# Twelve weight slabs a layer multiplied as 2x2 blocks with seven block products (Strassen's scheme), the block sums on GpSimd

## What is computed

```python
h = rms_norm(x, norm_g)
proj = h @ w_in                       # 1024 columns in, 7496 out
(sa_q, sa_k, sa_v, c_q, c_kv, k_pe, ds_q, ds_k, ds_v, ix_q, ix_k, ix_w,
 z_a, z_b, z_c, g) = jnp.split(proj, _split_points(IN_SIZES), axis=-1)
# y_a, y_b, y_c: three kinds of attention on the first twelve pieces
branches = jnp.stack([y_a * jax.nn.silu(z_a), y_b * jax.nn.silu(z_b), y_c * jax.nn.silu(z_c)], axis=2)
up = jnp.einsum('bsnc,ncd->bsnd', branches, w_branch)
gates = jax.nn.sigmoid(g.reshape(B, S, N_BRANCH, D) + gate_b)
merged = jnp.sum(gates * up, axis=2)
return x + merged @ w_out
```

## Time and profile before

| | |
|---|---|
| median of three runs | 1280.16 us (1278.92 to 1280.26) |
| the profiled execution's own time | 1282.07 us |
| its span in the profile | 1280.3 us |
| granted TensorE clock, share of full | 0.999 |
| TensorE, VectorE, ScalarE, GpSimd busy | 97%, 61%, 47%, 22% of the span |
| the stage of z, g and up slabs, first layer | about 364 to 604 us |

### The profile page before, as it was taken

The page is one execution under the profiler, slowest core; times in us unless marked ns, Lnnn a source line. Parts: engine busy times, 40 slices in busy tenths (PEclk is TensorE's granted clock), DMA queues, the critical chain, the costliest instruction groups (busy, mean ns, idle before and its releaser), DMA issues.

```text
span 1280.3 us, 17872 instructions
## 1 busy us (share of the span) xinstructions
PE 1238.8 (97%) x6478; PEld 945.5 (74%) x6478; DVE 778.6 (61%) x1603; ACT 595.9 (47%) x1109; POOL 275.5 (22%) x405
## 2 busy tenths in 40 slices
PE   6999999999999999999999999999989999999999
PEld 5776666565688888888887776665657888888887
DVE  6988878888742343444556477888874424434442
ACT  4457656766742232233245366677676323223330
POOL 1473222466800000000000032235673000000000
PEclk9999999999999999999999999999999999999999
DMA  7345112202514223233332312220133332332331
GB/s 210 102 131 132 34 37 47 66 1 62 156 48 131 92 85 92 95 99 99 99 99 67 99 33 67 50 67 1 42 96 96 114 93 89 109 93 95 99 99 66
DMA packets 123161, 108.55 MB, mean 85 GB/s; under 512 B 38849, under 2 KB 105793, under 8 KB 123074
## 3 DMA queue, kind: packets, MB, share of 16 engines
q1 hardware_dynamic: 123074, 107.41, 28.4%
HBM read 100.05 MB, written 7.34 MB: 84 GB/s over the span
## 4 chain that ended last, share of the span: by engine, by line
PE 75%; DVE 12%; ACT 6%; issue 4%; POOL 2%; SPq 1%; DMA 1%; DVEq 0%; ACTq 0%; POOLq 0%
PE bank L904 20%; PE bank L906 20%; PE bank L905 20%; DVE w_lo L777 3%; PE bank L1050 2%; PE bank L1244 2%; PE bank L1227 2%; PE bank L1260 2%; PE bank L860 1%; PE bank L1273 1%; DVE score L1987 1%; PE bank L1095 1%; ACT soft L1562 1%; ACT soft L1564 1%; PE bank L1233 1%
## 5 line engine op out<-in xcount | busy, mean ns | idle before, releaser
L904 PE MATMUL bank<-h_hi,w_hi 128*128 128x512 f32 (+1 forms) x928 | 361.5, 390 | 8.0 <-DVE w_lo L777 5.4
L906 PE MATMUL bank<-h_hi,w_lo 128*128 128x512 f32 (+1 forms) x928 | 352.2, 380 | 0.0
L905 PE MATMUL bank<-h_lo,w_hi 128*128 128x512 f32 (+1 forms) x928 | 352.0, 379 | 0.0
L777 DVE TENSOR_TENSOR w_lo<-raw,w_hi 128x2048 fp32r<-128x2048 f32 (+2 forms) x98 | 188.8, 1928 | 123.4 <-ACT w_hi L771 123.3
L904 PEld LDWEIGHTS bank<-h_hi,w_hi 128*128 128x128 f32 x928 | 175.2, 189 | 59.9 <-issue 16.9
L771 ACT CAST w_hi<-raw 128x2048 fp32r<-128x2048 f32 (+2 forms) x100 | 159.0, 1594 | 113.0 <-PE bank L906 110.1
L906 PEld LDWEIGHTS bank<-h_hi,w_lo 128*128 128x128 f32 x928 | 175.1, 189 | 33.2
L905 PEld LDWEIGHTS bank<-h_lo,w_hi 128*128 128x128 f32 x928 | 175.3, 189 | 32.0 <-issue 1.9
L1759 ACT ACTIVATE gate<-bank,gains 128x512 f32<-128x512 f32 x48 | 33.0, 688 | 166.3 <-PE bank L906 166.2
L1679 ACT ACTIVATE probs<-probs,stat 128x128 f32<-128x128 f32 (+3 forms) x128 | 71.4, 559 | 48.7 <-DVE stat L2153 32.5
L2409 POOL TENSOR_SCALAR probs<-probs,stat 128x128 f32<-128x128 f32 (+3 forms) x128 | 75.8, 596 | 65.0 <-DVE stat L2132 63.6
(11 more groups left out here) (253 smaller groups left out, 2173.8 us busy)
## 6 DMA issues: line engine op xcount, KB each, us to landing
raw<-in_w_in SPq DMA_DIRECT2D x56, 1024.0 KB, 5.2
raw<-in_w_branch SPq DMA_DIRECT2D x12, 1024.0 KB, 5.1
raw<-in_w_out SPq DMA_DIRECT2D x8, 1024.0 KB, 5.3
bias<-bias_dram SPq DMA_DIRECT2D x16, 256.0 KB, 2.8
bias<-bias_dram SPq DMA_DIRECT2D x16, 192.0 KB, 2.6
x_sb<-in_x SPq DMA_DIRECT2D x4, 512.0 KB, 5.3
bias_dram<-bias_out SPq DMA_DIRECT2D x8, 256.0 KB, 2.9
raw<-in_w_in SPq DMA_DIRECT2D x4, 512.0 KB, 4.8
```

The source lines that it names most:

```text
L777: e.tensor_tensor(w_lo[:, s % RING, a:b], raw[:, s % RAW, a:b], w_hi[:, s % RING, a:b].bitcast(F32), ALU.subtract).then_inc(*lo_signal(nam ...
L904: pe.matmul(out_ap, lh, rh, start=start and i == 0, stop=False)
L905: pe.matmul(out_ap, lh, rl, start=False, stop=False)
L906: mm = pe.matmul(out_ap, ll, rh, start=False, stop=stop and i == n - 1)
```

## The change

Twelve slabs of each layer (the list `SEVEN`: g0_2, g0_3, z1_0, z1_1, g1_0 to g1_3, z2_0, z2_1, g2_0, g2_1; these are names of slabs) are multiplied as 2x2 blocks. The slab is cut into four blocks of 512 inputs x 128 outputs (A11 to A22), the input into four of 512 inputs x 256 positions. Seven block products replace eight. Each product is 4 x 3 = 12 matmuls with 256 columns.

- **GpSimd** makes four sums of input blocks once a layer (`t_sum`, eight operations of 128x1024) and, for every one of the twelve slabs, four sums of weight blocks: S1 = A21 + A22, S2 = S1 - A11, S4 = A12 - S2, S3 = A11 - A21.
- **ScalarE** rounds the four input sums, and of each slab seven blocks of 128x512 in place of one slab of 128x2048 (`part_hi`); it copies the products after A11, S1 and S2 out of their banks (`keep`). These copies stand in its list among the roundings for the slab that follows.
- **VectorE** makes the remainders of the input sums and of the seven blocks (`part_lo`) and builds three blocks of the result from a bank and a copy (`add_block`): C11, C12, C22. The fourth, C21, stays in the bank; for z it is copied.
- **TensorE** works through the products in the order A11, S1, then the last product (A22) of the slab before, S2, A12, S4, S3. S2 waits for the copy of A11, the last product waits until C22 has been read.
- The rounded blocks lie in a ring of eight quarters. Since `t_sum` and its remainders take the place of x, **SP** loads x again after g2_1 (in the second layer from a copy in DRAM that it wrote at the layer's start).

Core of the diff:

```diff
+SEVEN = [f"g0_{j}" for j in (2, 3)] + [f"{n}_{j}" for n in ("z1", "g1", "z2") for j in range(4 if n[0] == "g" else 2)] + ["g2_0", "g2_1"]
+PARTS = ("A11", "S1", "S2", "A12", "S4", "S3", "A22")
 # TensorE
+                def multiply(name, part, b, start):
+                    pe.wait_ge(*dve_split.at(name, part))
+                    lh, ll = part_of(name, part), part_of(name, part, False)
+                    rh, rl = moving[part]
+                    for k in range(4):
+                        for i, (w, m) in enumerate(((lh, rh), (lh, rl), (ll, rh))):
+                            mm = pe.matmul(b[:, left], w[:, k, :], m[:, k, :], start=start and k == 0 and i == 0,
+                                           stop=k == 3 and i == 2, skip_group_check=not start)
+                    mm.then_inc(*product.tick(name, part))
+                def last_product(name):
+                    pe.wait_ge(*block_sum.at(name, "C22"))
+                    multiply(name, "A22", seven_banks(name)[0], False)
+                def seven(name):
...
+                    if i >= 2:
+                        pe.wait_ge(*last_block(SEVEN[i - 2]))
+                    else:
+                        pe.wait_ge(*gate_sig.at("g0_3"))
+                        pe.wait_ge(*t_split.at(3))
+                    multiply(name, "A11", b1, True)
+                    multiply(name, "S1", b3, True)
+                    if SLABS[SLAB_NO[name] - 1] in SEVEN:
+                        last_product(SLABS[SLAB_NO[name] - 1])
+                    pe.wait_ge(*product_kept.at(name, "A11"))
+                    multiply(name, "S2", b1, False)
+                    multiply(name, "A12", b2, True)
+                    pe.wait_ge(*product_kept.at(name, "S1"))
+                    multiply(name, "S4", b3, False)
+                    pe.wait_ge(*product_kept.at(name, "S2"))
+                    multiply(name, "S3", b1, False)
 # ScalarE, one slab
+                        keep(name, "A11", b1)
+                        for part in late[:1]:
+                            part_hi(e, name, part)
+                        next_hi(name, "S1")
+                        keep(name, "S1", b3)
...
+                        if before:
+                            second_tile(before)
+                        next_hi(name, "A11")
+                        keep(name, "S2", b1)
...
+                        next_hi(name, "S4")
+                        first_tile(name)
+                        next_hi(name, "S3")
+                        if name[0] == "z":
+                            br_split(e, n, m)
+                        next_hi(name, "A22")
...
+                    if name == "up2_0":
+                        split_hi(e, "g2_2")
 # VectorE, one slab
+                        add_block(name, "C11", "A12", b2, "A11")
...
+                        next_lo(name, "S4")
+                        add_block(name, "C12", "S4", b3, "S2")
+                        next_lo(name, "S3")
+                        add_block(name, "C22", "S3", b1, "S1")
+                        if name[0] == "z":
+                            z_product(n, m, gate[:, m, :])
+                        next_lo(name, "A22")
...
+                    if name == "up2_0":
+                        split_lo(e, "g2_2")
 # GpSimd
+                for k, name in enumerate(SEVEN):
+                    e.wait_ge(*raw_in[SLAB_NO[name] % RAW].at(name))
+                    for part, a, b, op in (("S1", "A21", "A22", ALU.add), ("S2", "S1", "A11", ALU.subtract),
+                                           ("S4", "A12", "S2", ALU.subtract), ("S3", "A11", "A21", ALU.subtract)):
+                        if k:
+                            e.wait_ge(*dve_split.at(SEVEN[k - 1], part))
...
 # SP
+                    if name == "up2_1":
+                        e.wait_ge(*product.at(SEVEN[-1], PARTS[-1]))
+                        for s in range(ST):
+                            src = x_dram[s * P:(s + 1) * P, :] if layer.l else x[0, s * P:(s + 1) * P, :]
+                            e.dma_start(x_sb[:, s, :], src).then_inc(*x_back.tick(s, by=16))
```

More of the change, by code:

```diff
@@ L687, in _ @@
                     load(name)
+                    if layer.l and name == "sa_k0":
+                        for s in range(ST):
+                            e.wait_ge(*x_new.before(1, s))
+                            e.dma_start(x_dram[s * P:(s + 1) * P, :], x_sb[:, s, :]).then_inc(*x_spilled.tick(s, by=16))
                 load("z0_0")
@@ L770, in split_hi @@
                 wait_ring_slot(e, name)
-            e.copy(w_hi[:, s % RING, a:b], raw[:, s % RAW, a:b]).then_inc(*hi_ready.tick(name, part or 0))
+            if part is not None or n < 4 * QUARTER or s < SLAB_NO["z0_0"]:
+                e.copy(w_hi[:, s % RING, a:b], raw[:, s % RAW, a:b]).then_inc(*hi_ready.tick(name, part or 0))
+                return
+            for a, b, slot, at in runs(name):
+                e.copy(w_hi[:, slot, at:at + b - a], raw[:, s % RAW, a:b]).then_inc(*hi_ready.tick(name, part or 0))
         def split_lo(e, name, part=None):
@@ L2250, in _ @@
+                nxt = SLAB_NO["out0_1"]
                 while nxt < NS - 1:
```

441 lines of the change are left out of this document (338 added, 103 removed).

## The result

The changed kernel takes 1378.23 us, the median of four runs (1375.74 to 1383.53), against 1279.62 (1278.92 to 1280.26) for the kernel before: a ratio of 1.0776, with a 95% interval from 1.0742 to 1.0810. Slower was forecast, 1340.5 with a range from 1295 to 1364; the time lies above the range. The direction and most of the mechanisms held, and 38 us were not in the sum.

What follows compares the result with a forecast made beforehand. The prediction took TensorE, busy for 97% of the span, to bound the kernel. Its terms, - 19.9 + 11.2 + 4.8 + 52 + 6 + 6.2 = + 60.3 on 1282.1, gave 1342.4, or 1340.5 us on the median's scale; range 1295 to 1364.

Steps and rivals of the forecast that it cites:

- seven products, 24 slabs: TensorE's block products: 84 steps of 0.1198 us replace 48 of 0.227, saving 0.83 us a slab, 19.9 us for 24 slabs.
- start of the stage: Before g0_0: VectorE's operations each wait behind GpSimd's input sums, so TensorE starts 5.6 us late; +11.2 us in two layers.
- g0_2: First slab of a layer by seven products: waits for the last input remainder, queued behind up0_0's last merge; 2.4 us, +4.8 together.
- four z runs: z1_0, z1_1, g1_0, g1_1 and the same for n = 2: VectorE's loop exceeds TensorE's time; 13 us each, +52.
- four g pairs: g0_2, g0_3 and g1_2, g1_3, without z work: waits from sums and the up slab's remainder, 1.5 us each, +6.
- up2_0: VectorE's remainder of g2_2 stands ahead of up2_0's tile products, so TensorE waits 3.1 us a layer; +6.2.
- ring at the start of layer 2: Quarters of the ring of rounded blocks were set at nothing, as lying beside TensorE's work.
- hold: VectorE instructions with two SBUF inputs and GpSimd ones reading SBUF exclude each other; without it, z runs 6.0 us over each.
- The rival in which the hold does not bind: VectorE keeps the port and GpSimd finds the gaps: 1295 us; hold partly or not binding (1295 to 1325), chance 0.20.
- the one in which the reserve of one slab holds: Rival: blocks are rounded a slab ahead and TensorE runs through; only g0_2 and up2_0 waits remain: 1270.7 us, chance 0.10.
- more than forecast: Rival: all terms at their upper ends and about 60 restarts, each 0.10 us dearer, give 1364 us; above that, chance 0.07.

## Why the prediction was wrong, and where it was right

Each term as a difference of the table's stretches, with 0.83 us a slab added back that seven products save and the pairs' last products counted with their pair, both layers together; the slow steps are taken out of the terms and stand by themselves.

| step of the prediction | forecast | measured |
|---|---|---|
| seven products, 24 slabs | - 19.9 | - 19.9 (taken as such) |
| start of the stage | + 11.2 | + 10.6 |
| g0_2 | + 4.8 | + 6.0 |
| four z runs | + 52 | + 49.6 |
| four g pairs | + 6 | + 10.2 |
| up2_0 | + 6.2 | + 6.5 |
| out0_0's remainder | not in it | + 7.9 |
| ring at the start of layer 2 | 0 | + 3.2 |
| steps at 1.2 GHz | not in it | + 22.7 |
| attention parts | 0 | - 3.1 |
| sum, against one profiled execution | + 60.3 | + 93.7 |

**The clock is the step that failed.** The sum took each gap at its length, with nothing for what follows it; only the upper bound of 1364 had 0.10 us for each of 60 restarts, a price read behind a wait that had hardly held TensorE up. At 22.7 us the slow steps are two thirds of the 33.4 that the sum misses of the profiled execution. The run with the filled gaps shows for six of the fourteen places, 8.4 us, that they follow TensorE's standing still and not the restart; the other eight places are read from the trace. The Trainium skill (TensorE: Matmul & The Clock Gate, Part 1) has it, under "The HAM clock gate", that a gate halves TensorE's clock when the engine has been idle. The rows agree: 0.50 in 482 to 486 us, behind a gap of 4.1.

**Two waits were left out.** The prediction saw that VectorE's remainder of g2_2 had come ahead of the tile products of up2_0, and priced it at 3.1 us (measured 3.25); that the same rewriting had put out0_0's remainder behind those of up2_1 it did not see: 3.9 us a layer. And "quarters of the ring lie beside TensorE's work" was wrong in the one place where the count of quarters matters, the seam between the layers: 3.2 us and 1.4 of slow steps.

**The g pairs** were set at 1.5 us within bounds of 0 and 2.6; the measured mean is 2.6. In part it is C22, whose place behind the next remainder cost 0.9 to 1.3 us a pair, as the run with C22 exchanged shows. In part it is the up slab's rounding, which waits for the ring: its last quarter is that of S2, and only then could 1.9 us of rounding and 2.3 of remainder begin. With the up slab rounded by quarters 0.5 to 0.7 us a pair of it went.

**Right, and for the reason given:** the start of the stage, where 5.6 was forecast and the gaps cost 5.3; the size of the z runs, 12.4 us each against 13, of which the forecast without hold was 6.0 and the run without sums gave 6.1 (both measured without slow steps; with them the z runs cost 15.6 each, over the upper bound of 15.2); the two waits named for them; 256-column steps of 0.12 us. The rival in which the hold does not bind is out by the 38 us of the run without sums, the one in which the reserve of one slab holds by the 9.6 us of waits for C22 and the copy in the first z1 run alone. That the 13 came so near is in part luck: it was picked between bounds of 6.0 and 15.2. The price of "more than forecast", 1364, was still too low, because it raised each term to its upper end and had no term for the clock.

## What to carry to other kernels

A gap on TensorE costs more than its length where it brings the clock down; price a forecast gap of the lengths met here (2 to 5 us) with the slow steps behind it too, 1.2 to 2.7 us a place, though not every such gap had them. Where a change makes four engines pass blocks round, look first for the stretch in which the busiest helper has room: the same seven products lost 29 us over twelve slabs with every order mended, and gained 4 over the four that had VectorE to themselves. And when a wait is taken away in a loop that another engine's lag sets, expect to meet it at the next hand-over.

## What the runs showed of the hardware

- The clock does not fall at every gap of a length. The gap of 3.0 us in up2_0 was followed by steps at full pace in the changed kernel's profile, in both layers; with the filled gaps 5 or 6 steps of double length followed it in the first layer and 13 in the second. Elsewhere steps went slow 1.5 us after TensorE had resumed, behind a gap of only 2.0 us (start, duration, instruction; the gap ends with the first row):

```profile
1163.89 0.39 PE L1475 MATMUL bank<-t_hi,w_hi 128*128 128x256 f32 x1 [1.99 <-DVE gate L2496]
1164.12 0.28 PE L1475 MATMUL bank<-t_lo,w_hi 128*128 128x256 f32 x1
...
1165.59 0.42 PE L1475 MATMUL bank<-t_lo,w_hi 128*128 128x256 f32 x1
1165.81 0.42 PE L1475 MATMUL bank<-t_hi,w_lo 128*128 128x256 f32 x1
```

- The time goes with it: the changed kernel's four runs spread over 0.6%, and the slowest has the lowest clock (1383.5 us at 0.968, the others 0.978 to 0.980), while the four of the kernel before beside them spread over 0.1%.
